# Norms taken one token tile after the other in a two-layer encoder kernel

## The reference, cut to what matters

```python
def rmsnorm(x, g):
    xf = x.astype(jnp.float32)
    y = xf * lax.rsqrt(jnp.mean(xf * xf, axis=-1, keepdims=True) + EPS)
    return (y * g.astype(jnp.float32)).astype(x.dtype)

for i in range(DEPTH):
    if i % N_MIXERS == 0:
        x = x + mlstm_mixer(x, *mix_params[i])
    else:
        x = x + diff_attn_mixer(x, positions, *mix_params[i], lambda_init=lambda_init)
    x = x + peer_ffn(x, *ffn_params[i])
```

## Time and profile before

| | us |
|---|---|
| median of 3 runs | 1866.83 (1865.65 to 1868.53) |
| the profiled execution | 1865.97 |
| its span, first to last instruction | 1864.2 |
| PE busy | 1847.5 (99%) |
| DVE busy | 1420.9 (76%) |
| ACT busy | 974.8 (52%) |

### The profile page before, as it was taken

The page is one execution under the profiler, slowest core; times in us unless marked ns, Lnnn a source line. Parts: engine busy times, 40 slices in busy tenths (PEclk is TensorE's granted clock), DMA queues, the critical chain, the costliest instruction groups (busy, mean ns, idle before and its releaser), DMA issues.

```text
span 1864.2 us, 32895 instructions
## 1 busy us (share of the span) xinstructions
PE 1847.5 (99%) x11242; PEld 1554.4 (83%) x11242; DVE 1420.9 (76%) x2599; ACT 974.8 (52%) x1394; POOL 105.8 (6%) x71
## 2 busy tenths in 40 slices
PE   8999999999999999999999999999999999999999
PEld 6778888888888888888887788888888888888887
DVE  5576688988888888655588757889888888885555
ACT  5475555654545444444467645565545544444443
POOL 0000341000000000000000014410000000000000
PEclk9999999999999999999999999999999999999999
DMA  6345555555555555555553355555555555556555
GB/s 231 135 136 160 162 187 191 181 172 170 167 177 172 180 177 170 193 187 195 192 185 119 115 181 170 182 179 183 180 175 172 180 169 173 176 172 194 198 190 171
DMA packets 89487, 326.15 MB, mean 175 GB/s; under 512 B 10064, under 2 KB 10192, under 8 KB 89040
## 3 DMA queue, kind: packets, MB, share of 16 engines
q1 hardware_dynamic: 88848, 323.00, 53.1%
q10 hardware_dynamic: 576, 2.33, 0.3%
HBM read 324.24 MB, written 1.05 MB: 174 GB/s over the span
## 4 chain that ended last, share of the span: by engine, by line
PE 95%; DVE 3%; ACT 1%; issue 0%; DMA 0%; ACTq 0%; DVEq 0%
PE ps L1531 25%; PE ps L1529 14%; PE ps L1776 13%; PE ps L1778 12%; PE ps L1777 12%; PE ps L1528 4%; PE ps L1724 3%; PE ps L1548 2%; PE ps L1550 2%; PE ps L1549 2%; DVE wl L848 1%; PE ps L1705 1%; PE ps L1668 1%; PE ps L1831 0%; PE ps L1861 0%
## 5 line engine op out<-in xcount | busy, mean ns | idle before, releaser
L848 DVE TENSOR_TENSOR wl<-raw,wh 128x1024 fp32r<-128x1024 f32 x569 | 697.1, 1228 | 158.4 <-ACT wh L477 149.6
L477 ACT ACTIVATE wh<-raw 128x1024 fp32r<-128x1024 f32 x609 | 641.7, 1055 | 312.3 <-PE ps L1778 164.9
L1531 PE MATMUL ps<-hT,wh 128*128 128x512 f32 x2072 | 739.3, 396 | 0.0
L1529 PE MATMUL ps<-hT,wl 128*128 128x256 f32 x2368 | 613.1, 279 | 0.0
L1529 PEld LDWEIGHTS ps<-hT,wl 128*128 128x128 f32 x2368 | 446.6, 189 | 25.1
L1531 PEld LDWEIGHTS ps<-hT,wh 128*128 128x128 f32 x2072 | 389.7, 188 | 79.4
L1776 PE MATMUL ps<-wh,hT 128*128 128x512 f32 x1024 | 402.1, 393 | 0.3 <-DVE big L832 0.2
L1778 PE MATMUL ps<-wh,hT 128*128 128x512 f32 x1024 | 399.2, 390 | 0.0
L1777 PE MATMUL ps<-wl,hT 128*128 128x512 f32 x1024 | 398.6, 389 | 0.0
L1778 PEld LDWEIGHTS ps<-wh,hT 128*128 128x128 f32 x1024 | 192.3, 188 | 40.6
L1776 PEld LDWEIGHTS ps<-wh,hT 128*128 128x128 f32 x1024 | 192.4, 188 | 39.5 <-issue 0.9
(11 more groups left out here) (226 smaller groups left out, 1327.2 us busy)
## 6 DMA issues: line engine op xcount, KB each, us to landing
raw<-stream SPq DMA_DIRECT2D x612, 512.0 KB, 3.5
big<-keys ACTq DMA_DIRECT2D x2, 1024.0 KB, 8.6
x<-x_in SPq DMA_DIRECT2D x1, 1024.0 KB, 5.6
out<-x SPq DMA_DIRECT2D x4, 256.0 KB, 2.1
sm<-small ACTq DMA_DIRECT2D x1, 228.5 KB, 5.8
pos_i<-positions ACTq DMA_DIRECT2D x1, 1.0 KB, 6.7
```

The source lines that it names most:

```text
L477: act.activation(wh[:, r, :], raw[:, r, :], ACT.Copy).then_inc(high_ready, 1)
L848: dve.tensor_tensor(wl[:, r, :], raw[:, r, :], wh[:, r, :].bitcast(F32), ALU.subtract).then_inc(made_low(unit), 1)
L1529: pe.matmul(near, w_l[:, kd, :], hTh[:, kd, :], start=False, stop=False)
L1531: i = pe.matmul(wide, w_h[:, kd, :], both, start=False, stop=(kd == KD - 1))
```

## The change

**Turns.** All four turns go tile by tile. DVE adds both halves of tile 0, then interleaves the variance, reciprocal and scaling of tile 0 with the adds of tile 1, and does tile 1's variance, reciprocal, scaling last. ACT takes two roots of one column in place of one of two. PE transposes the eight blocks of tile 0, runs 5 `keep_warm` multiplications (none in turn 0; the 10 or 16 in front are gone), then transposes the eight blocks of tile 1.

**Banks.** The transposed blocks now lie in four PSUM banks in place of eight: blocks kd and kd + 4 share a bank. So the transposition of block kd + 4 of tile 1 waits until `hTl` of block kd has been made. All 16 transpositions still stand in PE's program ahead of the first matmul of the next projection.

**Projections.** PE takes the last two units of `wo` together, and the last two of `v`: first tile 0 of both, then tile 1 of both. The parts of one unit (the third of `wq`) are made after the turn and no longer inside it.

**Softmax loop.** DVE's last step of the loop over 16 attention steps no longer calls `ahead`.

```diff
-        TURN_BANK = {0: (7, 4, 5, 6, 0, 1, 2, 3), 2: (4, 5, 6, 7, 0, 1, 2, 3), 3: (4, 5, 6, 7, 0, 1, 2, 3),
-                     5: (4, 5, 6, 7, 0, 1, 2, 3)}
+        TURN_BANK = {0: (4, 5, 6, 0), 2: (2, 3, 0, 5), 3: (6, 7, 0, 1), 5: (5, 6, 7, 2)}
...
-            ahead(unit_of["wo0"] + U_WO - 1)
+            ahead(unit_of["wo0"] + U_WO - 2)
...
+                add(0, 0)
+                add(0, 1)
+                variance(0)
+                add(1, 0)
+                factor(0)
+                add(1, 1)
+                scaled(0)
+                variance(1)
+                factor(1)
+                scaled(1)
...
-                ahead(unit_of["qkv"] + 15 + STEP_AT[j] // 4)
+                if j < 15:
+                    ahead(unit_of["qkv"] + 15 + STEP_AT[j] // 4)
...
-                for kd in range(KD):
-                    for t in range(NT):
+                for t in range(NT):
+                    if t == 1 and n > 0:
+                        keep_warm(4, 5)
+                    for kd in range(KD):
                         if kd in (0, KD // 2):
-                            pe.wait_ge(xn_ready, 4 * XN_TURN[n] + 2 * (kd // 4) + t + 1)
-                        i = pe.transpose(ps[:, TURN_BANK[n][kd], t * P:(t + 1) * P], xn[:, t, kd * P:(kd + 1) * P],
+                            pe.wait_ge(xn_ready, 4 * XN_TURN[n] + 2 * t + kd // 4 + 1)
+                        if t == 1 and kd >= 4:
+                            pe.wait_ge(hT_ready, 8 * n + kd - 3)
+                        at_ = kd // 4 * S + t * P
+                        i = pe.transpose(ps[:, TURN_BANK[n][kd % 4], at_:at_ + P], xn[:, t, kd * P:(kd + 1) * P],
                                          ident[:])
-                    i.then_inc(xT_ready, 1)
+                        if t == 1:
+                            i.then_inc(xT_ready, 1)
...
             def ffn(l):
-                keep_warm(4, 10)
                 transposes((2, 5)[l])
...
-                for r in range(U_E - TURN, U_E):
+                for r in range(U_E - TURN, U_E - 2):
                     down(r, None)
+                last = [split(first + r) for r in (U_E - 2, U_E - 1)]
+                pe.wait_ge(stage_ready, U_E // 2 * (l + 1))
+                for t in range(NT):
+                    for r in (U_E - 2, U_E - 1):
+                        i = down_half(last[r - U_E + 2], r, t, False)
+                        if t == 1:
+                            i.then_inc(used, 1)
...
-            keep_warm(4, 16)
             transposes(3)
```

More of the change, by code:

```diff
@@ L485, in norm, with root @@
             def norm(n, k):
-                order = [(0, 0), (1, 0), (0, 1), (1, 1)] if n in (2, 5) else [(0, 0), (0, 1), (1, 0), (1, 1)]
-                for i, (t, nb) in enumerate(order):
+                def root(t):
+                    act.wait_ge(var_ready, 2 * k + t + 1)
+                    act.activation(rstd[:, t:t + 1], var[:, t:t + 1], ACT.Sqrt).then_inc(std_ready, 1)
+                for i in range(2 * NT):
+                    t, nb = i // 2, i % 2
                     if n == 0:
@@ L812, in chain, with norm, variance, factor @@
                 dve.wait_ge(dve_step, steps[0])
[L814 to L821, removed]
-                    for t in range(NT):
+            def norm(n, k, add=lambda t, nb: None):
+                def variance(t):
+                    dve.wait_ge(ssq_ready, 4 * k + 2 * t + 2)
+                    dve.scalar_tensor_tensor(out=var[:, t:t + 1], in0=ssq[:, t, 0:1], scalar=EPS, in1=ssq[:, t, 1:2],
+                                             op0=ALU.add, op1=ALU.add).then_inc(var_ready, 1)
+                def factor(t):
+                    dve.wait_ge(std_ready, 2 * k + t + 1)
+                    chain(dve.reciprocal(var[:, t:t + 1], rstd[:, t:t + 1]))
+                def scaled(t):
+                    for nb in range(2):
                         half = slice(nb * 512, (nb + 1) * 512)
@@ L864, in gain, with add_to_x @@
                 return lambda kd: sm[:, SM_GAIN + g * KD + kd:SM_GAIN + g * KD + kd + 1]
[L866 to L872, removed]
+            def add_to_x(l, t, nb):
+                last = unit_of[f"wo{l}"] + U_WO - 2 + nb
+                if t == 0:
+                    ahead(unit_of[f"wo{l}"] + U_WO - 2)
+                    dve.wait_ge(wo_mm, 2 * l + nb + 1)
+                else:
+                    dve.wait_ge(used, last + 1)
+                dve.tensor_tensor(x[:, t, nb * 512:(nb + 1) * 512], x[:, t, nb * 512:(nb + 1) * 512],
+                                  ps[:, OUT_BANKS[l][nb] + t, :], ALU.add).then_inc(x_ready, 1)
             def head_var(part, k, scale, eps=None):
@@ L1462, in _ @@
                 heads_transposed(4, pair, da_scale)
-            add_to_x(1)
             ffn(1)
+            for t in range(NT):
+                for nb in range(2):
+                    sum_to_x(1, t, nb)
         @block.tensor
@@ L1541, in token_unit @@
                         before(t)
[L1542 to L1550, removed]
+                    i = token_half(w, q, t, out(t), between)
                     if q == 3 and t == 0:
@@ L1555, in out_projection @@
             def out_projection(l, n, ready):
-                for q in range(4):
+                first = unit_of[f"wo{l}"]
+                for q in range(3):
                     for nb in range(2):
@@ L1563, in out_projection @@
                             pe.wait_ge(*ready[nb])
-                        token_unit(unit_of[f"wo{l}"] + 2 * q + nb, q, lambda t: ps[:, OUT_BANKS[l][nb] + t, :], wo_mm)
+                        token_unit(first + 2 * q + nb, q, lambda t: ps[:, OUT_BANKS[l][nb] + t, :], wo_mm)
+                last = [split(first + U_WO - 2 + nb) for nb in range(2)]
+                for t in range(NT):
+                    for nb in range(2):
+                        i = token_half(last[nb], 3, t, ps[:, OUT_BANKS[l][nb] + t, :])
+                        i.then_inc(wo_mm if t == 0 else used, 1)
             pe.wait_ge(consts, CONSTS)
@@ L1761, in down @@
                 def down(r, turn):
-                    w_h, w_l = split(first + r, turn)
+                    w = split(first + r, turn)
                     if r % 2 == 0:
                         pe.wait_ge(stage_ready, offset(turn, TURN // 2, U_E // 2 * l + r // 2 + 1))
-                    fresh_bank = turn is None and r == 0
                     for t in range(NT):
[L1768 to L1780, removed]
@@ L1781, in down @@
+                        i = down_half(w, r, t, turn is None and r == 0)
                     i.then_inc(used, 1)
```

68 lines of the change are left out of this document (49 added, 19 removed).

## The result

| | before | after |
|---|---|---|
| median of 8 runs each, us | 1867.13 (1865.58 to 1868.55) | 1872.05 (1870.04 to 1873.49) |
| the profiled execution | 1865.97 | 1871.32 |
| its span | 1864.2 | 1869.5 |
| DVE busy | 1420.9 (76%) | 1422.3 (76%) |

The ratio is 1.0026, 95% interval 1.0015 to 1.0036: the change makes the kernel slower, by 4.9 us in the medians, or 0.26%. The forecast was 1870.7 in a range of 1867.3 to 1873.8.

A forecast was written before the change was run, and what follows sets the result against it. PE, busy 99% of the span, was taken to bound the kernel. Turn losses of 0.8 + 0.8 + 2.2 + 0.1 = 3.9 us put the profiled execution at 1869.9 and the median at 1870.7, range 1867.3 to 1873.8.

The forecast's parts named there:

- Turns 2 and 5: PE's first matmul waits behind block 7's transposition for the fourth low part; 0.8 us lost in each turn.
- Turn 3: Same wait, with a weight unit's low part ahead of the third `hTl`; 2.2 us lost, none given back by pacing.
- Turn 0: Same dependence at the program's start, without `keep_warm`, partly swallowed; 0.1 us lost, between -0.3 and +0.4.
- The waits together: Sum of the losses in turns 2, 5, 3 and 0: 3.9 us.
- the rival with one fall in turn 3: Granted clock falls in turn 3's thin 3.4 us, costing 1.7 us more: 1872.4; chance 0.25.
- Swallowed in the attention: Turn 3's loss only shortens PE's 2.2 us wait for DVE's copy; 1.7 us remain, 1868.5; chance 0.16.
- The clock in three turns: Granted clock falls in turns 2, 3 and 5, costing 3 x 1.7 = 5.1 us: 1875.8; chance 0.06.
- The faster rival: Low-part wait doesn't bind; turns gain up to 0.6 us each, 1.8 together: 1865.0; chance 0.10 for faster or equal.
- No cost: Program end, softmax step and removed `keep_warm` cost nothing; third `wq` unit's later parts likewise, with 1.7 us of cover.

The follow-up runs named there:

- e4: The changed kernel, with DVE making turn 3's weight-unit low parts behind all eight token low parts, not between them; 1870.68 us, ratio 1.0021 to the kernel before.
- e2: The kernel before with only the four PSUM banks and their waits for low parts, tile order as before; 1871.54 us, ratio 1.0032 to the kernel before.
- e1: The changed kernel with eight PSUM banks, no new waits, ten 256-column constant multiplications in place of five of 512; 1865.38 us, ratio 0.9994 to the kernel before.
- e3: The changed kernel without the five constant multiplications between the two tiles in turns 2, 3 and 5; 1874.25 us, ratio 1.0048 to the kernel before.
- e5: The kernel before with eight constant multiplications added in PE's wait in the attention; 1865.67 us, ratio 0.9997 to the kernel before.
- e7: e1 with six 256-column constant multiplications between the tiles in place of ten; 1865.34 us, ratio 0.9996 to the kernel before.
- e6: The changed kernel with eight constant multiplications added in PE's wait in the attention; 1871.36 us, ratio 1.0030 to the kernel before.
- e9: e7 with PE's last two units of `wo` and of `v` in their old order, unit by unit; 1868.62 us, ratio 1.0010 to the kernel before.
- e8: e7 with eight constant multiplications added in PE's wait in the attention; 1863.81 us, ratio 0.9989 to the kernel before.

## Why the prediction was right

**Turns 2 and 5**, 0.8 each: measured +0.88 and +0.89 to the start of the second unit, by the mechanism that was written down. First matmul at 142.97 (predicted 143.05), second unit at 145.82 (145.87), tile 1's scaling at 139.23 (139.27), the first low part at 141.15 (141.21). That the low parts aren't held by copies that wait for transpositions came true as well, though ACT's copies now wait for `hT_ready` too: the eight low parts still take 3.23 us. The pacing gave back 0.2, as worked out.

**Turn 3**, 2.2: measured +2.16, the first matmul at 944.79. It was predicted at 944.15 plus 0.9 from before it, 945.05. Its two parts are shown by themselves, in e4 and e2.

**Turn 0**, +0.1: the stretch up to turn 2 came out at -0.12. ACT's first square of `x` starts at 6.38 in before and at 6.19 in after, so counted from there it is +0.07 (130.37 and 130.44), as small as it was put. It is no absence of cost, though: with eight banks (e1, 6.22 and 136.24) it is 130.02. So the four banks cost 0.4 us in turn 0 as well. That before comes out as late as after has another reason, its order of tiles or the clock's fall at its start, and no run tells the two apart. The clock's fall of the earlier trace rows isn't in the profile of after, where the same stretch reads

```profile
10.30:13.60 3.30, 1.69 (x8) 1.00 1.02 377
```

Each of the two profiles thus has one fall of the clock, before at the start and after in the attention, and both have a mean of 0.999. What the fall at the start cost the kernel before isn't shown. In its profile the transpositions at 0.50 end at 13.59 and the first matmul starts at 13.66; in after the wait for the low parts holds it until 13.62; e1, with neither, starts it at 12.46. In e4, where the fall began only at 13.36 and caught the matmuls, turn 2 came 0.7 us later than in after, counted from the first square.

**The waits together** came to 3.8 us against the forecast's 3.9. The medians differ by 4.9 and the profiles by 5.4. In the profiles the rest is the clock, and in the medians it likely is. The clock was weighed as a rival of turns alone, and that was too narrow: after's profile has its fall in the attention (1.67 us), a place that the prediction read as safe from the page of before, whose digits of 9 can't show a fall of 3 us. Here luck helped. The median, 1872.05, lies nearer to the rival with one fall in turn 3 (1872.4) than to the forecast (1870.7), and the range that was made to hold that fall held one in another place. Whether the change makes the falls more frequent is likely, not shown: a mean of 0.998 stands in 6 of 8 runs of after, but also in 8 of 30, 10 of 22 and 8 of 15 of the kernel before on three chips, and one of 0.998 or below in 5 of 6 of e2.

**Swallowed in the attention**, 1868.5: refuted. PE reaches the wait 2.90 later (1034.87 against 1031.97) and leaves it 2.90 later (1037.40 against 1034.50), after 2.15 us both times. DVE's copy follows PE, as the argument against this rival said.

**The clock in three turns**, 1875.8: not in after, whose gaps all ran at 1.00. e3, at 1874.25, comes near it: take the five multiplications away and the mean clock goes to 0.994 to 0.996 in four of five runs. So the 1.1 us of `keep_warm` that the prediction named as its reason against the fall do hold the clock up. That the falls of e3 lie in turns 2 and 5 isn't shown; its profile has them behind turn 3 and in the attention.

The Trainium skill, "TensorE: Matmul & The Clock Gate", section "Part 4: PE-mode transpose", says that transpositions don't count as busy in the same way. The kernel before came up from 0.50 with nothing else running, which speaks against it, and so does e5's start: its 16 transpositions run from 9.99 to 13.32, and the clock was at 1.00 again before they had ended.

```profile
9.80:13.10 3.30, 3.10 (x14) 0.50 1.02 418
13.20:13.30 0.10, 0.10 (x3) 1.00 0.26 82
```

In e2's start the waits for the low parts break the row of 16, and there 0.50 lasted from 10.40 to 17.10, into the matmuls. What e3 adds is no proof for either side: its turns 2 and 5 kept 1.00 in the profile on 16 transpositions alone, in gaps of 5.89 us, while turn 3's matmuls fell to 0.53.

**The faster rival**, 1865.0 at no binding wait: the wait binds in after. It is a good description of e7 though, whose three turns gain 1.66 us with no such wait. e1 has none either, but gains only 0.09 to 0.15 in a turn, since its filler holds tile 1's transpositions as the prediction had worked out.

**No cost**: the third `wq` unit's parts behind the turn and the softmax step left no mark; between turn 2's second unit and turn 3's last matmul, and from turn 3 to the attention, the two kernels run in step to within 0.1 us.

## What to carry to other kernels

When two blocks of a pipeline are put into one buffer, ask not only whether the buffer will be free in time, but what stands behind the waiting instruction on its engine: here four transpositions that no one needed yet held up matmuls whose data was ready, 1 us each time, and what their releaser's engine does in between is added to it (1.14 us in turn 3). Whether four banks would have done with the first matmuls put ahead of the four waiting transpositions was not tried. A step that shortens a chain by half a microsecond shows only when the next resource in line is free, so look at the filler and the buffer limit together with it. The filler can't simply go, as e3 shows; a shorter one gave the gain in e7. Judge differences of 2 us in a kernel of 1866 by many runs with their mean clock beside them; one profile shows one draw.

## What the runs showed of the hardware

**The clock falls in some executions and not in others.** The same wait of 2.15 us with small matmuls around it left the clock at 1.00 in the profile of before and at 0.51 in that of after; turn 3, in which after and e6 have the same instructions, kept 1.00 in after and was followed by 0.50 in e6. The profiles show three places beside the one in e9: the start (before, e2, e4, e5), behind turn 3 (e3, e6), and the attention. In the attention it fell in five of the six profiled kernels that go tile by tile and have no filler there (after, e1, e3, e4, e7, not e9), in neither with the old order (before, e2), and in none of the three with the filler (e5, e6, e8). With one profile each this is a hint that the change matters for it, no more. Rows of e1 in the attention and of e2 at the start:

```profile
1034.00:1037.30 3.30, 3.30 (x18) 0.50 0.25 98
...
10.40:17.10 6.70, 6.03 (x28) 0.50 0.61 235
```

Apart from that last one each fall lasts 3.2 to 3.4 us. In after it cost 1.67.

**The count of such falls is a part of a kernel's spread, not all of it.** In e1 the runs with a mean of 1.000 have a median of 1863.88, those at 0.999 one of 1865.49, 1.6 apart. But e8's eleven runs are all at 1.000 and still range over 2.5 us, and in e5 the runs at 1.000 (1865.72) are no faster than those at 0.999 (1865.59).

**Eight multiplications in a wait can pay.** They take 1.89 us of idle time. e7 without them has a mean of 0.999 in seven of eleven runs, e8 with them 1.000 in all, with 1.5 us between the medians. That this came from e8's filler, and not from how those runs fell, is likely but was seen in that one pair; against the kernel before beside them e5 gained 0.5 us, within its spread, and e6 gained nothing over after.
